# Reordering the opening of a two-block transformer kernel: loads, modulation columns and the first two weight chunks

## The reference, cut to what matters

```
mod = silu(c) @ ada_w + ada_b                       # c: 1 x 1024, ada_w: 1024 x 9216
sh1, sc1, g1, ... = split(mod, 9)
u = x * (1 + sc1) + sh1                             # x: 512 x 1024
y = (silu(u @ ffn1_w_gate) * (u @ ffn1_w_up)) @ ffn1_w_down   # 1024 x 2816, 2816 x 1024
```

## Time and profile before

| | |
|---|---|
| median of 3 runs | 1920.85 us (1920.52 to 1923.37) |
| span of the profiled execution (no other time of it is listed) | 1921.3 us |
| PE busy | 1841.7 us, 96% |
| DVE, ACT, POOL busy | 55%, 43%, 26% |
| mean granted clock of TensorE | 0.981 |
| DMA traffic | 247.84 MB, mean 129 GB/s |

### The profile page before, as it was taken

The page is one execution under the profiler, slowest core; times in us unless marked ns, Lnnn a source line. Parts: engine busy times, 40 slices in busy tenths (PEclk is TensorE's granted clock), DMA queues, the critical chain, the costliest instruction groups (busy, mean ns, idle before and its releaser), DMA issues.

```text
span 1921.3 us, 23120 instructions
## 1 busy us (share of the span) xinstructions
PE 1841.7 (96%) x8960; PEld 1503.1 (78%) x8960; DVE 1055.2 (55%) x1078; ACT 818.5 (43%) x864; POOL 500.1 (26%) x644
## 2 busy tenths in 40 slices
PE   4999999999999899999999999998999999999998
PEld 3888888877888577787888888877998867877877
DVE  6455556566887987446332333369552436555552
ACT  3222223247666765326443332264222557333351
POOL 0411111031899483002000000050104995301100
PEclk8999999999999899999999999999989999999999
DMA  8455556463233134343223223354823422542411
GB/s 313 155 185 184 175 163 204 145 210 121 87 110 121 66 120 147 116 154 121 88 87 109 87 75 98 90 176 171 157 85 133 128 71 65 158 161 91 143 44 44
DMA packets 204214, 247.84 MB, mean 129 GB/s; under 512 B 5899, under 2 KB 184875, under 8 KB 202091
## 3 DMA queue, kind: packets, MB, share of 16 engines
q1 hardware_dynamic: 185643, 171.27, 28.1%
q0 software_dynamic: 13472, 51.42, 9.3%
q10 hardware_dynamic: 5024, 24.12, 3.4%
HBM read 227.39 MB, written 19.40 MB: 128 GB/s over the span
## 4 chain that ended last, share of the span: by engine, by line
PE 71%; POOL 9%; DVE 8%; ACT 6%; issue 4%; DMA 2%; SPq 1%; DVEq 0%; ACTq 0%; POOLq 0%
PE ps L2093 21%; PE ps L2287 18%; PE ps L2159 11%; POOL conv_out L487 8%; PE ps L2123 3%; ACT w_hi L604 3%; PE ps L2428 2%; PE ps L2469 2%; PE ps L2624 2%; DVE ada_acc L1322 2%; PE ps L2542 1%; DVE w_lo L1224 1%; PE ps L2457 1%; DMA w_raw<-in_ffn_w_gate 1%; PE ps L2478 1%
## 5 line engine op out<-in xcount | busy, mean ns | idle before, releaser
L1224 DVE TENSOR_TENSOR w_lo<-w_raw,w_hi 128x2048 fp32r<-128x2048 f32 x158 | 369.8, 2341 | 554.2 <-ACT w_hi L604 552.1
L604 ACT ACTIVATE w_hi<-w_raw 128x2048 fp32r<-128x2048 f32 x156 | 298.4, 1913 | 664.3 <-PE ps L2287 244.6
L2093 PE MATMUL ps<-u_hi,w_hi 128*128 128x512 f32 x656 | 261.2, 398 | 10.0 <-DVE w_lo L1224 10.0
L2093 PE MATMUL ps<-u_lo,w_hi 128*128 128x512 f32 x656 | 257.7, 393 | 0.0
L2093 PE MATMUL ps<-u_hi,w_lo 128*128 128x512 f32 x656 | 257.5, 393 | 0.0
L2287 PE MATMUL ps<-u_hi,w_hi 128*128 128x512 f32 x656 | 257.0, 392 | 0.0
L2287 PE MATMUL ps<-u_lo,w_hi 128*128 128x512 f32 x656 | 256.0, 390 | 0.0
L2287 PE MATMUL ps<-u_hi,w_lo 128*128 128x512 f32 x656 | 255.8, 390 | 0.0
L487 POOL TENSOR_TENSOR conv_out<-conv_out,conv_tap 128x512 f32<-128x512 f32 x120 | 195.7, 1631 | 80.6 <-ACT conv_tap L787 63.5
L2093 PEld LDWEIGHTS ps<-u_hi,w_hi 128*128 128x128 f32 x656 | 124.8, 190 | 38.7 <-DVE w_lo L1224 7.0
L2093 PEld LDWEIGHTS ps<-u_lo,w_hi 128*128 128x128 f32 x656 | 124.9, 190 | 26.5 <-issue 1.0
(11 more groups left out here) (505 smaller groups left out, 3297.1 us busy)
## 6 DMA issues: line engine op xcount, KB each, us to landing
w_raw<-in_w_in SPq DMA_DIRECT2D x44, 1024.0 KB, 5.2
ada_raw<-in_ada_w POOLq DMA_DIRECT2D x56, 512.0 KB, 4.9
w_raw<-in_ffn_w_gate SPq DMA_DIRECT2D x22, 1024.0 KB, 5.4
w_raw<-in_ffn_w_up SPq DMA_DIRECT2D x22, 1024.0 KB, 5.3
w_raw<-in_ffn_w_down SPq DMA_DIRECT2D x32, 704.0 KB, 4.6
ada_first<-in_ada_w SPq DMA_DIRECT2D x8, 1024.0 KB, 14.3
w_raw<-in_w_out SPq DMA_DIRECT2D x8, 1024.0 KB, 5.1
w_raw<-in_xa_wk SPq DMA_DIRECT2D x4, 1024.0 KB, 5.3
```

The lines of the kernel that those rows point to most:

```text
L604: A(WHI[:, slot], WRAW[:, slot], ACT.Copy).then_inc(s["w_hi"], 1)
L1224: V.tensor_tensor(WLO[:, slot], WRAW[:, slot], WHI[:, slot].bitcast(F32), ALU.subtract).then_inc(s["w_lo"], 1)
L2093: ins = M(PS[:, 2 * j + t, 0:n], w[:, j, at_:at_ + P], a[:, k, 0:n], start=(k == 0 and q == 0), stop=(k == KT - 1 and q == 2))
```

## The change

SP begins with the scale slices; the four constant loads go to ScalarE's queue. x and the shift slices are loaded in halves of 512 columns. The shift steps are 8 on the first half and 8 on the second, so ADA_STEPS = 24 steps are counted. Chunk (0,0) and (0,1) are worked on in one stretch, k by k, with the transposes of the upper half of x and the columns of the upper shift half between the steps. The full-precision u of the opening comes from ScalarE instead of VectorE. The low part of chunk (0,1) is made before the first UL, not after the last. The parameter transposes stand behind both chunks.

```diff
@@ sync @@
-            sp.dma_start(IDENT[:], I["const_ident"]).then_inc(s["consts_load"], 16)
-            sp.dma_start(CONSTC[:], I["const_cols"]).then_inc(s["consts_load"], 16)
-            rows(0, 0, row(I["ada_b"]), 72)
-            rows(0, 72, I["c"].rearrange("a (r p) -> (a r) p", p=P), 8)
...
-            ada_slices(0)
-            sp.dma_start(XN[:], I["x"][0].rearrange("(t p) d -> p t d", p=P)).then_inc(s["x_load"], 16)
+            for q in range(4):
+                sp.dma_start(ADI[:, 0, 2 * q:2 * q + 2], wk8(I["ada_w"])[:, 2 * q:2 * q + 2, D:2 * D]).then_inc(ada_scale[q], 16)
...
-                ada_slices(1)
                 load(0, None, 0, wk8(wg)[:, :, 0:256], True)
+                x_half(0)
                 load(1, None, 0, wk8(wu)[:, :, 0:256], True)
+                for q in range(4):
+                    shift_slice(q, 0).then_inc(ada_shift[q], 16)
+                sp.wait_ge(s["x_load"], 16)
+                x_half(1)
+                for q in range(4):
+                    sp.wait_ge(ada_scale[q], 16)
+                    shift_slice(q, 1).then_inc(ada_scale[q], 16)
                 parameter_rows()
@@ gpsimd: ADA_FIRST becomes ADA_STEPS in the waits on ada_step @@
@@ scalar @@
+            def first_modulated(first, last, shifts):
+                act.wait_ge(s["modx_ready"], 1)
+                act.wait_ge(s["mod_ready"], shifts)
+                act.wait_ge(s["x_ready"], last)
+                for f in range(first, last):
+                    scale, bias = MODX[:, f:f + 1], MOD[:, SH1 + f:SH1 + f + 1]
+                    A(UH[:, f], X[:, f], ACT.Identity, scale=scale, bias=bias).then_inc(s["uh_ready"], 1)
+                    if f >= 2:
+                        act.wait_ge(s["ul_ready"], f - 1)
+                    A(UT[:, f % 2], X[:, f], ACT.Identity, scale=scale, bias=bias).then_inc(s["ut_ready"], 1)
...
+            act.dma_start(PST[72:80, 0, :], I["c"].rearrange("a (r p) -> (a r) p", p=P)).then_inc(s["consts_load"], 16)
+            act.dma_start(IDENT[:], I["const_ident"]).then_inc(s["consts_load"], 16)
+            act.dma_start(PST[0:72, 0, :], I["ada_b"].rearrange("(r p) -> r p", p=P)).then_inc(s["consts_load"], 16)
+            act.dma_start(CONSTC[:], I["const_cols"]).then_inc(s["consts_load"], 16)
...
             first_hi(0)
-            act.wait_ge(s["modx_ready"], 1)
-            act.wait_ge(s["mod_ready"], 2)
-            modulate_hi(0, lambda f: MODX[:, f:f + 1], lambda f: MOD[:, SH1 + f:SH1 + f + 1])
+            x_tiles(0, 4)
             first_hi(1)
+            first_modulated(0, 4, 2)
+            x_tiles(4, 8)
+            first_modulated(4, 8, 3)
             for g in range(1, 5):
                 act.wait_ge(s["param_t"], 5)
@@ vector @@
+            def first_modulated_lo(f):
+                dve.wait_ge(s["ut_ready"], f + 1)
+                dve.wait_ge(s["uh_ready"], f + 1)
+                V.tensor_tensor(UL[:, f], UT[:, f % 2], UH[:, f].bitcast(F32), ALU.subtract).then_inc(s["ul_ready"], 1)
...
-            ada_first_part(0)
+            ada_first_steps(0, slice(0, D), ada_scale, 16, 0)
             mod_cols(8, 16, 8)
             dve.wait_ge(s["mod_ready"], 1)
             derived(0, SC1, False).then_inc(s["modx_ready"], 1)
-            ada_first_part(1)
             lo(0, 0)
-            mod_cols(0, 8, 16)
...
-            modulate_lo(0, lambda f: MODX[:, f:f + 1], lambda f: MOD[:, SH1 + f:SH1 + f + 1])
+            ada_first_steps(1, slice(0, L), ada_shift, 16, 8)
+            mod_cols(0, 4, 12)
             lo(1, 1)
+            for f in range(4):
+                first_modulated_lo(f)
+                ada_first_steps(1, slice(L, D), ada_scale, 32, 16, 2 * f, 2 * f + 2)
+            mod_cols(4, 8, 16)
+            for f in range(4, KT):
+                first_modulated_lo(f)
@@ tensor @@
-            mod_first(0)
-            pe.wait_ge(s["x_load"], 16)
-            for f in range(KT):
...
+            mod_first(0, 0, 8, 8)
+            x_tiles(0, 4)
             pe.wait_ge(s["mod_ready"], 1)
-            mod_first(1)
+            mod_first(1, 0, 4, 16)
...
+                def first_chunks():
+                    for k in range(3):
+                        first_step(0, k)
+                        first_step(1, k)
+                        if k:
+                            x_tiles(2 * k + 2, 2 * k + 4)
+                    first_step(0, 3)
+                    pe.wait_ge(s["mod_ready"], 2)
+                    mod_first(1, 4, 8, 24)
+                    first_step(1, 3)
+                    first_step(0, 4)
+                    first_step(0, 5)
+                    first_step(1, 4)
+                    first_step(0, 6)
+                    first_step(0, 7)
+                    for k in range(5, KT):
+                        first_step(1, k)
...
                 if with_ada:
-                    first_chunk()
+                    first_chunks()
                     parameter_columns()
-                    chunk(0, 1)
```

More of the change, by code:

```diff
@@ L289, in build_program @@
         ada_load = (s["ada_load0"], s["ada_load1"])
-        ada_first = [[s[f"ada_{part}{q}"] for q in range(4)] for part in ("sc", "sh")]
+        ada_scale, ada_shift = ([s[f"ada_{part}{q}"] for q in range(4)] for part in ("sc", "sh"))
         free = (s["free0"], s["free1"])
@@ L302, in rows, with shift_slice, x_half @@
             def rows(g, r0, src, n):
-                sp.dma_start(PST[r0:r0 + n, g, :], src).then_inc(s["param_load" if g else "consts_load"], 16)
+                sp.dma_start(PST[r0:r0 + n, g, :], src).then_inc(s["param_load"], 16)
             row = lambda v: v.rearrange("(r p) -> r p", p=P)
-            sp.dma_start(IDENT[:], I["const_ident"]).then_inc(s["consts_load"], 16)
-            sp.dma_start(CONSTC[:], I["const_cols"]).then_inc(s["consts_load"], 16)
-            rows(0, 0, row(I["ada_b"]), 72)
-            rows(0, 72, I["c"].rearrange("a (r p) -> (a r) p", p=P), 8)
[L311 to L315, removed]
-            ada_slices(0)
-            sp.dma_start(XN[:], I["x"][0].rearrange("(t p) d -> p t d", p=P)).then_inc(s["x_load"], 16)
+            for q in range(4):
+                sp.dma_start(ADI[:, 0, 2 * q:2 * q + 2], wk8(I["ada_w"])[:, 2 * q:2 * q + 2, D:2 * D]).then_inc(ada_scale[q], 16)
+            def shift_slice(q, half):
+                cols = slice(half * L, half * L + L)
+                return sp.dma_start(ADI[:, 1, 2 * q:2 * q + 2, cols], wk8(I["ada_w"])[:, 2 * q:2 * q + 2, cols])
+            def x_half(half):
+                cols = slice(half * L, half * L + L)
+                sp.dma_start(XN[:, :, cols], I["x"][0].rearrange("(t p) d -> p t d", p=P)[:, :, cols]).then_inc(s["x_load"], 16)
             def parameter_rows():
@@ L2225, in rms_sums, with mod_first @@
                     M(PS[:, 7], ONES[:], SQ[:, f % 2], start=False, stop=(f == KT - 1)).then_inc(s["sq_used"], 1)
-            def mod_first(part):
-                pe.wait_ge(s["ada_step"], 8 * part + 8)
-                for j in range(8):
+            def mod_first(part, first, last, steps):
+                pe.wait_ge(s["ada_step"], steps)
+                for j in range(first, last):
                     c = 8 * (1 - part) + j
@@ L2242, in _, with x_tiles @@
             pe.wait_ge(s["set_ready"], 5)
-            mod_first(0)
-            pe.wait_ge(s["x_load"], 16)
-            for f in range(KT):
-                if f >= 2:
-                    pe.wait_ge(s["x_ready"], f - 1)
-                for t in range(TT):
-                    ins = nc.tensor.transpose(PS[:, 6 + f % 2, t * P:(t + 1) * P], XN[:, t, f * P:(f + 1) * P], IDENT[:])
-                ins.then_inc(s["x_t"], 1)
+            mod_first(0, 0, 8, 8)
+            def x_tiles(first, last):
+                pe.wait_ge(s["x_load"], 16 if first < 4 else 32)
+                for f in range(first, last):
+                    if f >= 2:
+                        pe.wait_ge(s["x_ready"], f - 1)
+                    for t in range(TT):
+                        ins = nc.tensor.transpose(PS[:, 6 + f % 2, t * P:(t + 1) * P], XN[:, t, f * P:(f + 1) * P], IDENT[:])
+                    ins.then_inc(s["x_t"], 1)
+            x_tiles(0, 4)
             pe.wait_ge(s["mod_ready"], 1)
-            mod_first(1)
+            mod_first(1, 0, 4, 16)
             def parameter_columns():
```

67 lines of the change are left out of this document (32 added, 35 removed).

## The result

The changed kernel takes 1935.05 us, median of 4 runs (1934.04 to 1935.89); the kernel before 1922.11 in the same comparison. The ratio is 1.0068, with a 95% interval of 1.0056 to 1.0080: 13 us slower. The forecast was 1924.0, with a range up to 1927.0; the sign was that of its slower side, the size was four times as large.

The account below looks back on a forecast made before the run. TensorE, busy 96% of the span, was taken as the bound. Its start 5.2 earlier shrinks to 1.9 after both chunks; the exposed gap and clock put chunk (1,1)'s end 3.2 later: 1920.85 + 3.2 = 1924.0, range 1920.8 to 1927.0.

Parts of the forecast that it names:

- slower side: Whole kernel: the cases that end measurably slower, together given 0.42, against same 0.53 and faster 0.05.
- Start of the scale sum: Opening, VectorE: constants on ScalarE's queue land at 4.5, so the sum starts at 6.7 and ends at 16.8.
- second rival: Opening: constants land late, at 6.0 giving 1925.5, at the bound of 8.5 giving 1928; chance 0.12.
- the prediction's own sign: First matmul of chunk (0,0): prediction is wrong if TensorE starts before 33 or after 37; 34.65 was forecast.
- The path from there to the end of both chunks: Scale sum at 6.7, TensorE's start at 34.65, then chunks (0,0) and (0,1) until 62.7 instead of 64.57.
- the gap before step (0,4): Inside the first two chunks: TensorE waits 1.2 for the second half's shift columns behind step (0,3).
- the forecast's transfer times: Opening, SP's queue: slices landed by 13.5, then gate, input, up and half slices at 16.5, 19.1, 22.1 and 27.3.
- What was hidden comes out: Before chunk (1,0): transposes behind both chunks leave a gap of 5.1, then a clock fall costing 2.2.
- The wait of the first round for ada columns: Between chunks (1,0) and (1,1): the wait of 0.95 goes, and the clock fall behind it, 1.6.
- third and fourth rivals: Before chunk (1,0): no clock fall in the gap, 1923.2, chance 0.12; start's 5.2 kept whole, 1915.7, chance 0.05.
- first rival: Inside the first two chunks, at 47 to 52: clock falls once more, price 1.6, giving 1925.6; chance 0.18.
- The second round: Chunks (2,0) and (2,1) with what belongs to them: no term, nothing taken to be touched behind chunk (1,1).

Follow-up runs that it names:

- e5: Changed kernel, SP issuing only scale slice 0 and holding slices 1 to 3 until the four constants have landed: 1933.10 us, ratio 1.0049.
- e10: Changed kernel, SP waiting until the four constants have landed before it issues any slice: 1933.34 us, ratio 1.0049.
- e4: Kernel before, with only its four constant loads moved to ScalarE's queue: 1927.82 us, ratio 1.0021.
- e6: Changed kernel, const_cols moved to SP's parameter rows, so the first transpose waits for three loads: 1933.08 us, ratio 1.0050.
- e1: Changed kernel, the four constant loads back at the head of SP's queue: 1930.64 us, ratio 1.0038.
- e2: Changed kernel, the four parameter transposes moved from behind both first chunks to before step (0,6): 1928.07 us, ratio 1.0027.
- e11: Kernel before, with only the four parameter transposes moved behind chunk (0,1): 1929.42 us, ratio 1.0033.
- e8: As e7, with POOL issuing two loads of ada group 1 behind three of eight x scalings: 1919.51 us, ratio 0.9986.
- e7: Changed kernel, constants first on SP, second half's column passes earlier, chunk (0,0) finished first from k = 4, parameter transposes behind step (0,5): 1921.99 us, ratio 0.9992.
- e3: Changed kernel, constants first on SP's queue and parameter transposes before step (0,6): 1923.67 us, ratio 1.0000.
- e9: As e8, with c and identity heading SP's queue, ada_b on ScalarE's, const_cols among the parameter rows: 1919.56 us, ratio 0.9982.

## Why the prediction was wrong, point by point

**Start of the scale sum: failed.** "Now they share the engines with 4 MB: not before 3.7, and not later than slice 1, 8.5. I take 4.5, near the row." They landed at 10.51, outside both ends. The upper end was the error of method: nothing in the rows excluded that a small load waits longer than two slices. What decides is the bulk that is issued at the same time (e5, e10, e4): 4.03 with nothing, 6.58 beside 1 MB, 10.4 to 10.5 beside 4 MB; with three loads in place of four it was 9.10 (e6). The second rival named the mechanism and its consequence ("each microsecond goes into the end"), with 0.12, and priced it at 1928 at the worst. The miss is 6.0 at the scale sum, 5.8 at the first matmul, 6.0 at the end of (1,1). So this one term is the larger part of the error, and the prediction's own sign of it came: TensorE starts behind 37.

**The path from there to the end of both chunks: right, in part untested.** From the start of the scale sum to the first matmul 27.7 (forecast 27.95); from there to the parameter transposes 28.0 (forecast 28.05), with the gap before step (0,4) at 1.07 (1.2). But in the changed kernel VectorE waits for no slice on the way, so the forecast's transfer times were not put to the test; in e1, where it does, the first stretch takes 29.0. The late constants hid this, and the close agreement of 27.7 is luck to that extent.

**What was hidden comes out: right.** The gap is 5.01 (5.1) with the clock at 0.50 behind it, and from the first parameter transpose at 68.46 to the end of (1,1) are 30.8 (30.6). e2 and e11 confirm cause and size. The wait of the first round for ada columns is gone, as forecast.

**The third and fourth rivals** are out: the clock did fall, in the changed kernel and in e11. The first rival (a fall inside the first chunks, to be decided from a gap of about 1) did not occur: the gap was 1.07, the clock stood at 1.00 from 55 to 58, and the 48 matmuls behind the gap took 11.2. But a fall behind the ada wait of the second round did, at 113.

**The second round: a missing term.** "I take that moment as the end of chunk (1,1), the fourth of ffn1: from there on nothing is touched." That was wrong. The second round costs 2.8 more, a longer wait for the ada columns and the fall of the clock behind it. POOL's ada loads go out 24.6 behind the parameter transposes (24.4 before), and these now stand only 30.8 before the end of (1,1), not 37.0. That is 6.0 + 2.8 + 3.2 = 12.0 at the end of (2,1), 125.32 against 113.34, and 11.5 in the spans. With the transposes inside (e2) the round takes 23.3 again, and in e8, with two of the loads issued earlier, VectorE's wait is gone. But the distance alone does not give the 2.8: e11 has it too and lost 0.3, since its loads took 4.3 and not 6.7 to land. The wait for the columns in this round was 0.6 in e11, 1.1 in e7, 1.3 in e1, 1.5 in the changed kernel and 2.0 in e5; the clock fell behind the last three only, and the round cost 0.3, 0.8, 2.6, 2.8 and 4.9 more than the 23.2 of before. So a few tenths decide here; and the length of the wait isn't all, since in the first round of e2 the clock fell behind one of 1.15.

**The range** took the constants' worst case as 8.5 and left it out at its top end. An honest top for "never seen beside bulk" would have been the time at which all four slices are through.

## What to carry to other kernels

Small loads on which the chain of the opening depends have to be issued ahead of the bulk; another queue is no substitute for that. Issued on ScalarE's queue while the slices went out on SP's, they landed at 10.4 to 10.5. Issued 0.4 or more ahead of the slices, they landed at 3.3 to 4.2, though the first slice went out 1.2 to 1.6 before that: on SP's queue in e1, e3, e7 and e8, on both in e9. Waiting until they have landed (e10) is more than is needed, and delays the slices by 3.1. An instruction that only gathers parameters is not free where it is put: here, four transposes, 0.55 us together, held ScalarE's next split and with it 5 us of TensorE and the clock. When several stages hide behind each other (split, ada sum, POOL's scaling), shortening the cover in front of one lays bare the next, so each has to be counted against the new distance.

## What the runs showed of the hardware that I had not expected

Four loads of together 120 KB need 1.7 us behind the last issue alone and 8.1 beside 4 MB. The Trainium skill, page "DMA: Bandwidth & Descriptors", section "Queues, rings and completion order", says that each of the DMA engines takes turns between queues by packets. The order of e10, e5 and the changed kernel (4.03, 6.58, 10.51) fits that, as does e6, but no run here separates turns by packet from another sharing rule; in e6 37% fewer packets came with only 12% less time behind the last issue.

Issued ahead of the 4 MB by 0.4, the same four loads took 1.7 behind their last issue too (2.21 to 3.88 in e1).

PEclk is no proof of the level at the start of a kernel. In the windows of the changed kernel above it is 1.00 at 42, where a matmul of 512 columns goes out every 0.43 us, and 1.00 at 46, where it goes out every 0.23; in the kernel before the same pace of 0.43 stands beside 0.50. There the count of matmuls in a window tells the level.
